# Tokens of the expert slots: one-hot products on TensorE in place of a table scattered to DRAM and loaded back

## What is computed

```python
g_sel = argmax(xf @ w_router_group + b_router_group)         # one group of 4
e_in_group = (xf @ w_router_expert + b_router_expert)[g_sel] # its 8 experts
top_v, top_i = lax.top_k(e_in_group, 2)
e_id = g_sel[:, None] * EXPERTS_PER_GROUP + top_i
...
xb = xt[tok]                                                 # rows gathered for one expert
hb = jax.nn.silu(xb @ w_exp_gate[e]) * (xb @ w_exp_up[e])
yb = (hb @ w_exp_down[e]) * wt[:, None]
out = jnp.zeros_like(xt).at[buf_tok].add(yb)
```

## Time and profile before

| | |
|---|---|
| median of 3 runs | 1144.09 us (1141.61 to 1148.47) |
| the profiled execution | 1143.9 us, its span 1142.3 us |
| TensorE busy | 946.5 us (83%), mean granted clock 0.945 |
| VectorE, ScalarE, GpSimd busy | 334.4, 207.2, 215.4 us |
| DMA | 283.75 MB, mean 248 GB/s |
| routing and expert stage | from about 590 us to 1108 us of the span |
| one expert's x gather, y scatter | 128 rows x 512 float32 each, 0.262 MB |
| a weight load of an expert | 2048 KB = 2.097 MB |

### The profile page before, as it was taken

One profiled execution on the slowest core, in us unless ns is written; L12 is line 12 of the kernel. 1 busy time (PEld: TensorE's weight loads), 2 busy tenths in 40 slices (PEclk: granted clock), 3 DMA queues, 4 the chain that ended last, 5 costly groups with the idle time before them and its releaser, 6 DMA issues.

```text
span 1142.3 us, 11534 instructions
## 1 busy us (share of the span) xinstructions
PE 946.5 (83%) x4386; PEld 506.6 (44%) x4386; DVE 334.4 (29%) x722; ACT 207.2 (18%) x450; POOL 215.4 (19%) x328
## 2 busy tenths in 40 slices
PE   3987999999999998899967399787877778877770
PEld 3644444777776566674543143233333323323320
DVE  1069999983341112230152000000000000000006
ACT  4143111213344323000121001000000000000012
POOL 2750551100001200000234121111111111111113
PEclk9998999899999999899987699999999999999995
DMA  6940112421204528903046779999999999999947
GB/s 212 391 181 1 35 67 90 136 95 71 75 1 148 205 90 260 369 15 145 37 166 224 276 301 425 424 423 422 424 426 425 424 423 424 422 425 426 418 168 245
DMA packets 56830, 283.75 MB, mean 248 GB/s; under 512 B 13640, under 2 KB 14360, under 8 KB 37839
## 3 DMA queue, kind: packets, MB, share of 16 engines
q1 hardware_dynamic: 45591, 246.23, 54.3%
q0 software_dynamic: 11200, 37.00, 9.0%
HBM read 267.40 MB, written 23.18 MB: 254 GB/s over the span
## 4 chain that ended last, share of the span: by engine, by line
PE 61%; DVE 18%; issue 8%; DMA 5%; ACT 4%; SPq 2%; POOL 1%; POOLq 0%; ACTq 0%; DVEq 0%
PE psum L994 19%; PE psum L1009 10%; PE psum L756 8%; DVE arena L1385 6%; DVE arena L1383 6%; PE psum L910 5%; PE psum L590 3%; PE psum L892 3%; DMA arena<-in_w_branch_pool 2%; PE psum L1002 1%; PE psum L844 1%; DVE arena L1602 1%; PE psum L810 1%; ACT arena L1287 1%; ACT arena L1283 1%
## 5 line engine op out<-in xcount | busy, mean ns | idle before, releaser
L994 PE MATMUL psum<-arena 128*64 128x512 f32 x992 | 235.9, 630 | 56.9 <-issue 56.1
L994 PEld LDWEIGHTS psum<-arena 128*64 128x64 f32 x992 | 85.4, 145 | 205.8 <-issue 205.8
L1009 PE MATMUL psum<-arena 128*64 128x512 f32 x512 | 119.1, 606 | 18.1 <-ACT arena L1287 18.1
L756 PE MATMUL psum<-arena 128*128 128x288 f32 x480 | 124.4, 411 | 0.0
L590 PE MATMUL psum<-arena 128*128 128x512 f32 (+2 forms) x320 | 120.0, 534 | 2.1 <-ACT arena L1152 2.1
L756 PEld LDWEIGHTS psum<-arena 128*128 128x128 f32 x480 | 88.5, 190 | 30.4 <-issue 8.1
L1602 DVE TENSOR_TENSOR arena<-arena,psum 128x256 f32<-128x256 f32 x32 | 13.5, 421 | 289.8 <-ACT arena L1283 278.4
L1283 ACT ACTIVATE arena<-psum 128x256 f32<-128x256 f32 x32 | 12.3, 383 | 417.7 <-PE psum L994 404.8
L590 PEld LDWEIGHTS psum<-arena 128*128 128x128 f32 (+1 forms) x320 | 57.5, 206 | 55.0 <-issue 52.3
L1009 PEld LDWEIGHTS psum<-arena 128*64 128x64 f32 x512 | 41.0, 139 | 74.4 <-issue 74.4
L1606 DVE COPY arena<-psum 128x512 f32<-128x512 f32 x32 | 22.1, 691 | 176.5 <-PE psum L1009 176.5
(11 more groups left out here) (247 smaller groups left out, 910.9 us busy)
## 6 DMA issues: line engine op xcount, KB each, us to landing
arena<-in_w_exp_down SPq DMA_DIRECT2D x32, 2048.0 KB, 22.9
arena<-in_w_exp_gate SPq DMA_DIRECT2D x31, 2048.0 KB, 18.5
arena<-in_w_exp_up SPq DMA_DIRECT2D x30, 2048.0 KB, 22.5
arena<-in_w_in SPq DMA_DIRECT2D x8, 2048.0 KB, 8.1
y_d<-arena SPq DMA_DIRECT2D x1, 8192.0 KB
arena<-in_x_prompt SPq DMA_DIRECT2D x8, 512.0 KB, 6.8
arena<-in_w_out SPq DMA_DIRECT2D x2, 2048.0 KB, 7.8
arena<-in_w_exp_up SPq DMA_DIRECT2D x4, 1024.0 KB, 16.8
```

The lines of the kernel that those rows point to most:

```text
L756: last = pe.matmul(bank(2 + n % 2 if n < SAMPLE_G else 2, HN), ring[slot % 2][:, k, m * P:(m + 1) * P], xnT[:, k, HN * hh:HN * hh + HN], s ...
L994: last = pe.matmul(bank(2 + s, 512, rows).rearrange("p (w n) -> p w n", w=2), x_k, wgu[s][:, :, DE * k + 256 * q:DE * k + 256 * q + 256], ...
L1009: last = pe.matmul(bank(4 + s, 512, slice(64 * half, 64 * half + 64)), hT[s][:, k % 2, CAP * (k // 2):CAP * (k // 2) + CAP], wd[s][:, k, 5 ...
```

## The change

The index columns of all 32 experts now come from the one-hot products, so that GpSimd's table is not needed unless the overflow branch is taken; the scatters moved into that branch, and the load back with its four operations is gone.

```diff
-    parts["rowx"] = 2 * parts["tok"] - ABSENT
+    parts["rowx"] = np.where(parts["tok"] < NT, 2 * parts["tok"] - ABSENT, 0)
...
             for i in range(TILES):
-                for e in range(2):
+                for k in range(2):
                     for half in range(2):
-                        last = pe.matmul(bank(5 + e, 1, slice(CAP * half, CAP * half + CAP)), onehot[:, i, e, :], const("rowx")[:, i:i + 1],
-                                         start=(i == 0), stop=(i == TILES - 1))
+                        last = pe.matmul(bank(5, NE, slice(CAP * half, CAP * half + CAP)), onehot[:, i, k, :], t32[5 * k][:, i, :],
+                                         start=(i == 0 and k == 0), stop=(i == TILES - 1 and k == 1))
             last.then_inc(S["tok_done"], 1)
...
+            over_e = [P, TILES, NE]
+            dve.wait_ge(S["a_ready"], 1)
+            dve.tensor_tensor(t32[0], t32[3], const("rowx").unsqueeze(2).to_broadcast(over_e), ALU.mult)
+            dve.tensor_tensor(t32[5], t32[4], const("rowx").unsqueeze(2).to_broadcast(over_e), ALU.mult)
             dve.wait_ge(S["rank_done"], 1)
             rank = bank(4, TILES * NE).rearrange("p (t e) -> p t e", e=NE)
-
-            link(dve.scalar_tensor_tensor(t32[1][:, :, 0:2], ab[:, :, 0:2], -1000.0, rank[:, :, 0:2], ALU.mult, ALU.add))
-            for e in range(2):
-                ins = dve.scalar_tensor_tensor(onehot[:, :, e, :], iota[:, 0:CAP].unsqueeze(1).to_broadcast([P, TILES, CAP]), -1000.0,
-                                               t32[1][:, :, e:e + 1].to_broadcast([P, TILES, CAP]), ALU.add, ALU.is_equal)
+            dve.tensor_tensor(t32[1], rank, t32[3], ALU.mult)
+            link(dve.tensor_tensor(t32[2], rank, t32[4], ALU.mult))
+            dve.tensor_reduce(r1, t32[1], AX, ALU.add)
+            link(dve.tensor_reduce(r2, t32[2], AX, ALU.add))
+            for k, r in enumerate((r1, r2)):
+                ins = dve.tensor_tensor(onehot[:, :, k, :], iota[:, 0:CAP].unsqueeze(1).to_broadcast([P, TILES, CAP]),
+                                        r.unsqueeze(2).to_broadcast([P, TILES, CAP]), ALU.is_equal)
             ins.then_inc(S["oh_ready"], 1)
...
+            for hot, r, sl in ((t32[3], r1, s1), (t32[4], r2, s2)):
+                dve.tensor_tensor(t32[1], hot, const("base").unsqueeze(1).to_broadcast(over_e), ALU.mult)
...
+                if hot is t32[3]:
+                    dve.wait_ge(S["tok_done"], 1)
+                    dve.tensor_scalar(sidx2, bank(5, 2), const("lift"), None, ALU.add).then_inc(S["tok_out"], 1)
+                    dve.tensor_scalar(rowx, bank(5, NE), const("lift"), None, ALU.add)
+                    link(dve.tensor_scalar(rowy, bank(5, NE), 0.0, float(ABSENT), ALU.is_ge, ALU.mult))
+                    dve.tensor_tensor(rowy, rowy, const("rowy"), ALU.add).then_inc(S["tok_out"], 1)
...
+            pool.wait_ge(S["tok_out"], 1)
             for e in range(2):
-                pool.wait_ge(S["tok_out"], e + 1)
                 gather_x(e, M[e]["xg_in"])
 
-            pool.wait_ge(S["dest_ready"], 1)
-            pool.wait_ge(S["zero_st"], 16)
-            pool.wait_ge(S["tri_ready"], 2)
-            for i in range(TILES):
-                r = rows_of(i)
-                for k in range(2):
-                    pool.indirect_dma_start(tab_d, bass.IndirectOffsetOnAxis(ap=dest[0:r, k, i:i + 1], axis=0),
-                                            toki[0:r, i:i + 1], None).then_inc(S["sc_st"], 16)
-            pool.wait_ge(S["sc_st"], 16 * 2 * TILES)
...
-            pool.wait_ge(S["slots_in"], 32)
-            pool.tensor_scalar(rowx, slots, float(ABSENT), 2.0, ALU.min, ALU.mult)
...
+            pool.wait_ge(S["tok_out"], 2)
             with pool.Fori(1, NE // 2) as i:
```

More of the change, by code:

```diff
@@ L288, in program @@
         RT = o
-        t32 = [at(o + j * 160, TILES, NE) for j in range(5)]; o += 800
-        gmax, least, top1, top2, vdf, vex, gw, s1, s2, w1, w2, w_lo, w_hi = (at(o + j * TILES, TILES) for j in range(13)); o += 13 * TILES
+        t32 = [at(o + j * 160, TILES, NE) for j in range(6)]; o += 960
+        gmax, least, top1, top2, vdf, vex, gw, s1, s2, w1, w2, w_lo, w_hi, r1, r2 = (at(o + j * TILES, TILES) for j in range(15)); o += 15 * TILES
         ghot, gsh, gex = (at(o + j * TILES * EG, TILES, EG) for j in range(3)); o += 3 * TILES * EG
@@ L316, in program @@
         assert TILES * 2 * CAP <= D and 2 * CAP == P
-        sidx = [arena[:, o + s:o + s + 1].bitcast(I32) for s in range(2)]; o += 2
+        sidx2 = arena[:, o:o + 2].bitcast(I32); o += 2
+        sidx = [sidx2[:, s:s + 1] for s in range(2)]
         syid = [arena[:, o + s:o + s + 1].bitcast(I32) for s in range(2)]; o += 2
-        slots = arena[:, o:o + NE].bitcast(I32); o += NE
         rowx, rowy = at(o, NE), at(o + NE, NE); o += 2 * NE
@@ L1571, in _ @@
[L1571 to L1579, removed]
+            for hot, r, sl in ((t32[3], r1, s1), (t32[4], r2, s2)):
+                dve.tensor_tensor(t32[1], hot, const("base").unsqueeze(1).to_broadcast(over_e), ALU.mult)
+                link(dve.tensor_tensor(t32[2], hot, const("jump").unsqueeze(1).to_broadcast(over_e), ALU.mult))
+                dve.tensor_reduce(sl, t32[1], AX, ALU.add)
+                link(dve.tensor_reduce(gmax, t32[2], AX, ALU.add))
+                dve.tensor_tensor(sl, sl, r, ALU.add)
+                link(dve.scalar_tensor_tensor(gmax, r, CAP - 0.5, gmax, ALU.is_gt, ALU.mult))
+                link(dve.tensor_tensor(sl, sl, gmax, ALU.add))
+                if hot is t32[3]:
[4 more added lines that the diff above has]
+                    dve.tensor_tensor(rowy, rowy, const("rowy"), ALU.add).then_inc(S["tok_out"], 1)
@@ L1773, in _ @@
             link(pool.memset(xg[1], 0.0))
+            pool.wait_ge(S["tok_out"], 1)
             for e in range(2):
-                pool.wait_ge(S["tok_out"], e + 1)
                 gather_x(e, M[e]["xg_in"])
-            pool.wait_ge(S["dest_ready"], 1)
-            pool.wait_ge(S["zero_st"], 16)
-            pool.wait_ge(S["tri_ready"], 2)
-            for i in range(TILES):
-                r = rows_of(i)
-                for k in range(2):
-                    pool.indirect_dma_start(tab_d, bass.IndirectOffsetOnAxis(ap=dest[0:r, k, i:i + 1], axis=0),
-                                            toki[0:r, i:i + 1], None).then_inc(S["sc_st"], 16)
-            pool.wait_ge(S["sc_st"], 16 * 2 * TILES)
-            with nc.allow_non_contiguous_dma(reason="the slots' tokens, a column for each expert"):
-                for half in range(2):
-                    pool.dma_start(slots[CAP * half:CAP * half + CAP, :],
-                                   tab_d[0:FIRST, :].rearrange("(e c) a -> c (e a)", c=CAP)).then_inc(S["slots_in"], 16)
-            pool.wait_ge(S["slots_in"], 32)
-            pool.tensor_scalar(rowx, slots, float(ABSENT), 2.0, ALU.min, ALU.mult)
-            link(pool.tensor_scalar(rowy, slots, float(NT), float(ABSENT), ALU.is_ge, ALU.mult))
-            pool.tensor_tensor(rowx, rowx, const("half").to_broadcast([P, NE]), ALU.add)
-            link(pool.tensor_tensor(rowy, rowy, const("rowy"), ALU.add))
+            pool.wait_ge(S["tok_out"], 2)
             with pool.Fori(1, NE // 2) as i:
@@ L1828, in _ @@
                     pool.wait_ge(M[s]["y_done"], NE // 2)
+                pool.wait_ge(S["zero_st"], 16)
+                pool.wait_ge(S["tri_ready"], 2)
+                for i in range(TILES):
+                    r = rows_of(i)
+                    for k in range(2):
+                        pool.indirect_dma_start(tab_d, bass.IndirectOffsetOnAxis(ap=dest[0:r, k, i:i + 1], axis=0),
+                                                toki[0:r, i:i + 1], None).then_inc(S["sc_st"], 16)
+                pool.wait_ge(S["sc_st"], 16 * 2 * TILES)
                 pool.memset(zeros, 0.0).then_inc(S["zero_w"], 1)
```

5 lines of the change are left out of this document (2 added, 3 removed).

## The result

The changed kernel takes 1127.18 us (median of 4 runs, 1126.02 to 1127.66). The ratio to the kernel before, whose median stood at 1146.28 us over 4 runs by then, is 0.9852 with a 95% interval of 0.9817 to 0.9888. That is 13 to 21 us; the forecast was 1127 us, from 17.2 us off. Two executions on record, one of the kernel before (1447.41 us) and one of the kernel with a hold behind gather 2 (1656.33 us), ran at a mean granted clock of 0.65 and 0.56, and no median here counts them. The kernel before scatters by some 8 us in these four runs and by 14 us in 19 later ones (1137.14 to 1151.22), and part of the scatter is where the routing begins: in the profiled runs of this text the first rank product starts anywhere from 596.94 to 601.38 us.

The account below looks back on a forecast made before the run. The expert stage was taken as bound by the weight stream, which ran empty because expert 2's gather waited for a table. -19.0 + 0.97 + 0.5 + 0.3 = -17.2 us gave 1127 us, range 1122 to 1135.

Parts of the forecast that it names:

- The wait goes, and with it the empty stream: Before expert 2's turn: TensorE's 16.67 us wait for the gather vanishes, so g5 comes 19.0 us earlier by TensorE.
- my sum: Whole kernel: -19.0 + 0.97 + 0.5 + 0.3 = -17.2 us.
- VectorE's +0.97 us: Between rank and one-hots: two products and two sums added, one small operation gone, +0.97 us.
- The multiplications: VectorE ahead of its wait for the rank: two, some 0.6 us, hidden under TensorE's rank products.
- my three: TensorE's 32-column one-hot products: nothing if columns hide under weight loads, 0.4 us if the longer counts, 2.75 if they add.
- The stream level with TensorE: At g5: the weight stream is free 0.2 us after TensorE, taken as 0.3; 1.8 us late at 406 GB/s.
- my own list: Trace signs: right includes a full stream from 625 us; wrong includes a new TensorE wait for weights before expert 4.
- first rival: Before g5: gain lost to a stream at 340 GB/s, 8.3 us gained, 1136 us; chance 0.09.
- no gain of its own: Stream from 630 to 635 us: the table's load back slows it to 185 GB/s, already counted in the 19.5 us.
- The second's condition: Expert 2's or 3's rows come late, needing 20 us from issue to use, 7.8 the worst seen; rival's chance 0.06.
- The third's price: Routing before expert 0: every added us delays the kernel; costed at 1.5 us, slower only at 19; chance 0.02.
- The interference of VectorE with the gathers: First two gathers: a skill rule says each could lose one VectorE operation; trace bounds it at 0.1 us, left out.

Follow-up runs that it names:

- hold behind gather 2: Changed kernel with GpSimd held about 27 us by 47 zeroings of a scratch tile after issuing expert 2's gather; 1134.22 us.
- filler on TensorE: Changed kernel with 4 more unread products of 512 columns per expert ahead of its down products; 1135.87 us.
- hold of 10 us: Changed kernel with GpSimd zeroing a scratch tile 18 times between the two first gathers and its expert loop; 1126.63 us.
- traffic alone: Changed kernel with ten scatters and two table loads issued behind expert 2's early gather, their results unused; 1135.60 us, 535.0 from rank to end.
- hold of 29: Changed kernel with GpSimd zeroing a scratch tile 51 times between the two first gathers and its expert loop; 1145.16 us, 545.0 from rank to end.
- the warmed one: Changed kernel with experts 0 and 1 indexed first by the old operations, plus unread TensorE products in two waits; 1124.16 us.
- scatters alone: Changed kernel with the ten table scatters put back behind expert 2's early gather, without the table loads; 1128.50 us.

## Why the prediction was right, step by step

**The wait goes, and with it the empty stream.** Right, and shown by its own undoing: the wait without the table gives the old time (545.0 and 544.7 us from rank to end). g5 came 77.1 us behind the rank and now comes 59.1: 18.0 us earlier, with 17.2 in my sum. From g5 to the end of the span it is 467.6 us before and 467.8 after, so what g5 gains the end gains. The thirteen traces say it more sharply, 407.5 to 408.5 us from g5 to expert 30's gate_up, and the filler on TensorE confirms that the rest is the stream's.

**What is luck in the number.** From expert 1's turn to g5 the gain is 18.3 us (57.3 to 39.0), where my sum has 19.0 - 0.3 = 18.7. Ahead of that turn the kernel loses 1.16 us to the added operations, where I had 1.47, but expert 0's gate_up took 8.54 us in place of 9.43. These 0.9 us lie inside what this gate_up scatters from run to run (8.41 to 10.08 us, last section), and I don't credit them to the change; without them g5 comes 17.1 us earlier. That the median meets the forecast to 0.2 us is luck too: I took it off a median of 1144.09 us, and the same kernel's medians lie from 1142.5 to 1146.3.

**The added operations.** VectorE's +0.97 us was right to the hundredth: the one-hot products begin 1.90 us behind the rank before and 2.87 after. The multiplications were hidden. TensorE's products with 32 columns cost 2.35 us against 2.30, which is the case of my three in which the columns hide under the weight loads (in the kernel before these loads alone are busy for 2.21 of the 2.30 us). I had taken 0.5 us, and 0 was the bound. The flag was there at 606.93, before the turn began at 608.59. In all the first turn is 1.16 us further behind the rank.

**The stream level with TensorE.** Right within its bounds of 0 and 1.8 us: 0.82 us of wait for weights where I had 0.3 us of lateness. By my own list two signs came out against me, both small: a new wait of TensorE for weights ahead of expert 4, this one, and a stream that isn't full from 625 us on. The stretch from 625 to 630 moves only 320 GB/s, at a DMA share of 0.85. In the kernel with a hold of 10 us, also without the table's traffic, it moves 340 GB/s at 0.91, so the 340 of the first rival's row was not the table's alone. It did not last: from 630 to 645 us the rate was 430 to 435 GB/s, and the rival fell.

**The table's traffic as "no gain of its own".** Right in the kernel before, where the traffic ran while everything waited, but it must not be read as free. Four kernels make a square: wait and traffic 544.7, wait alone 545.0, traffic alone 535.0, neither 527.0 us. The traffic costs nothing beside the wait, to a us or two, and 8 us without it. A version that had moved the table off the gather's way and kept it would have given some 10 of the 18 us, if its traffic came at the time of this experiment's.

**The rivals.** The second's condition, 20 us from issue to use, was never near: with the gather 8.6 us later there was still no wait, 12.6 us from issue to use. The rows took longer than the 7.8 us that I called the worst, though: 8.9 us with the hold of 29 and 8.6 with the one behind gather 2, from issue to TensorE's turn. The third's price per us was right (3.1 for 3.1); it had no 19 us to work with. The interference of VectorE with the gathers: they take 1.12 and 1.01 us, against 1.11 and 1.01 before, so there is no trace of it.

## What to carry to other kernels

A stage that is bound by a stream still loses time where the stream runs empty. Add up the bytes by stretch against the steady rate, look for who holds the next load, and give a stall its price in the stream's missing bytes, not in the waiting engine's time. Costs in such a place don't add up: once a wait is gone, traffic that hid behind it has a price, and TensorE can pay for a wait a second time with its clock. Of an indexed path, ask which consumer comes first, and have an experiment hold it by a known time; two or three such holds find the spare time and the price behind it.

## What the runs showed of the hardware

- The scatter of single words can slow big loads although it moves next to nothing: in the one trace with the scatters alone, 576 tokens twice, 4 bytes each, cost the stream about 1.4 us and brought the weights that TensorE waited for 2.6 us later.
- What a wait costs a second time isn't a fixed share of it. Waits of 3.4 and 6.3 us before a gate_up made it 8.78 and 9.90 us long, against 7.09 after 0.8 us. But from 645 us on the thirteen traces have 377 gate_ups of 32 records. The 197 with less than 2 us of wait before them took 7.05 to 7.09 us, and of the 173 with 2.5 to 4 us of wait 111 took 8.40 to 10.09 and 62 still 7.09. Before a turn, 6.2 us of wait cost 1.6 us in the two turns and the down behind it, and 16.67 us cost 2.7 us. So a difference of up to 3 us behind such a wait can be chance.
- The same gate_up of expert 0 took 8.41 to 10.08 us in the twelve profiled runs other than the warmed one, with the same 0.77 us of wait right before it. Differences below some 1.5 us need more than one profile if they lie across that place.
- A float32 product with 64 columns of weights costs the same 58 to 59 ns a record with 1 or 32 columns to stream, at the low clock (0.50).
